# Two transformer blocks in one kernel: 64-column matmuls inside the 256-column projections, fillers among first tiles, and the second sparse selection spread over the first block's attention pieces

## What is computed

```python
def dsa_mixer(h, w_in, w_out, ...):
    q, k, v, qi, ki, wi = jnp.split(h @ w_in, cuts, axis=-1)
    ...
    logits = jnp.einsum('bthd,bsd->bths', qib, ki)
    score = jnp.einsum('bths,bth->bts', jax.nn.relu(logits), wib)
    _, sel = lax.top_k(jnp.where(visible, score, -jnp.inf), top_k)   # top_k = 64
    s = jnp.einsum('btgrd,btkgd->btgrk', qg, kg) * scale
    p = jax.nn.softmax(jnp.where(sel_ok, s, -jnp.inf), axis=-1)
    return jnp.einsum('btgrk,btkgd->btgrd', p, vg) @ w_out

def squared_relu_mlp(h, w_up, w_down):
    a = jax.nn.relu(h @ w_up)
    return (a * a) @ w_down

def swiglu(h, w1, w3, w2):
    return (jax.nn.silu(h @ w1) * (h @ w3)) @ w2
```

## Time and profile before

| | us |
|---|---|
| median of 3 runs | 1652.6 |
| the three runs | 1651.94, 1652.6, 1661.68 |
| the profiled execution, its own time | 1659.97 |
| its span | 1658.2 |
| PE busy in it (matmul) | 1611.2 |

### The profile page before, as it was taken

The page is one execution under the profiler, slowest core; times in us unless marked ns, Lnnn a source line. Parts: engine busy times, 40 slices in busy tenths (PEclk is TensorE's granted clock), DMA queues, the critical chain, the costliest instruction groups (busy, mean ns, idle before and its releaser), DMA issues.

```text
span 1658.2 us, 30920 instructions
## 1 busy us (share of the span) xinstructions
PE 1611.2 (97%) x12608; PEld 1535.0 (93%) x12608; DVE 1015.6 (61%) x1247; ACT 764.7 (46%) x1004; POOL 22.9 (1%) x39
## 2 busy tenths in 40 slices
PE   7989999999999999999999999999999999999999
PEld 5868999998999998999977999989999897889998
DVE  7786665568666546556467665466664657576653
ACT  4335554347655444444345444454443435554443
POOL 0000000004000000000000000000000000000000
PEclk9999999999999999999999999999999999899999
DMA  6701566644256665556623557635566351246573
GB/s 166 179 26 50 179 185 192 182 139 138 77 177 186 195 188 163 177 173 185 180 71 102 177 177 197 172 113 177 177 191 170 116 180 56 77 135 192 179 210 95
DMA packets 347106, 252.95 MB, mean 153 GB/s; under 512 B 32622, under 2 KB 345868, under 8 KB 347036
## 3 DMA queue, kind: packets, MB, share of 16 engines
q1 hardware_dynamic: 345424, 250.00, 51.2%
q10 hardware_dynamic: 1612, 1.97, 0.4%
HBM read 250.90 MB, written 1.05 MB: 152 GB/s over the span
## 4 chain that ended last, share of the span: by engine, by line
PE 86%; DVE 8%; ACT 2%; DMA 2%; issue 1%; ACTq 0%; SPq 0%; DVEq 0%
PE acc L531 26%; PE acc L533 25%; PE acc L532 25%; DVE w_low L1634 1%; ACT w_high L1147 1%; PE spare L714 1%; PE acc L556 1%; PE acc L736 1%; PE spare L556 1%; PE acc L722 1%; DVE xg_low L1678 1%; PE acc L1047 1%; DVE x_state L1841 1%; PE spare L588 1%; DVE evac_a L1839 1%
## 5 line engine op out<-in xcount | busy, mean ns | idle before, releaser
L1634 DVE TENSOR_TENSOR w_low<-w_raw,w_high 128x2048 fp32r<-128x2048 f32 (+2 forms) x222 | 528.6, 2381 | 381.9 <-ACT w_high L1147 381.9
L1147 ACT ACTIVATE w_high<-w_raw 128x2048 fp32r<-128x2048 f32 (+2 forms) x222 | 441.2, 1987 | 617.5 <-PE acc L533 598.6
L531 PE MATMUL acc<-xg_high,w_high 128*128 128x272 f32 (+2 forms) x2320 | 665.8, 287 | 13.3 <-DVE xg_low L1678 10.6
L533 PE MATMUL acc<-xg_high,w_low 128*128 128x272 f32 (+2 forms) x2320 | 657.4, 283 | 0.0
L532 PE MATMUL acc<-xg_low,w_high 128*128 128x272 f32 (+2 forms) x2320 | 657.4, 283 | 0.0
L531 PEld LDWEIGHTS acc<-xg_high,w_high 128*128 128x128 f32 (+1 forms) x2320 | 437.8, 189 | 23.6 <-issue 10.9
L532 PEld LDWEIGHTS acc<-xg_low,w_high 128*128 128x128 f32 (+1 forms) x2320 | 436.4, 188 | 2.5 <-issue 1.7
L533 PEld LDWEIGHTS acc<-xg_high,w_low 128*128 128x128 f32 (+1 forms) x2320 | 436.3, 188 | 0.2
L531 PE MATMUL acc<-hidden_high,w_high 128*128 128x256 f32 (+1 forms) x1216 | 343.7, 283 | 1.9 <-DVE w_low L1634 1.9
L533 PE MATMUL acc<-hidden_high,w_low 128*128 128x256 f32 (+1 forms) x1216 | 343.2, 282 | 0.0
L532 PE MATMUL acc<-hidden_low,w_high 128*128 128x256 f32 (+1 forms) x1216 | 343.1, 282 | 0.0
(11 more groups left out here) (284 smaller groups left out, 1455.1 us busy)
## 6 DMA issues: line engine op xcount, KB each, us to landing
w_raw<-in_ffn_w_dram SPq DMA_DIRECT2D x88, 1024.0 KB, 5.3
w_raw<-in_ffn_w_dram SPq DMA_DIRECT2D x32, 1408.0 KB, 6.9
w_raw<-in_mlp_w_up_dram SPq DMA_DIRECT2D x32, 1024.0 KB, 5.5
w_raw<-in_mlp_w_down_dram SPq DMA_DIRECT2D x32, 1024.0 KB, 5.5
w_raw<-in_attn_w_qkv_dram SPq DMA_DIRECT2D x12, 1024.0 KB, 5.1
w_raw<-in_a_w_in_dram SPq DMA_DIRECT2D x18, 256.0 KB, 4.4
w_raw<-in_a_w_in_dram SPq DMA_DIRECT2D x4, 1024.0 KB, 7.8
w_raw<-in_a_w_out_dram SPq DMA_DIRECT2D x4, 1024.0 KB, 5.0
```

Of the source, the lines that this page charges most:

```text
L531: pe.matmul(dst, high_w, high, start=first, stop=False)
L533: return pe.matmul(dst, low_w, high, start=False, stop=last)
L1147: act.activation(whi[slot(c)][:, 0:SIZES[c]], raw[c % 2][:, 0:SIZES[c]], ACT.Copy).then_inc(S["w_high"], 1)
L1634: dve.tensor_tensor(wlo[slot(c)][:, s], raw[c % 2][:, s], whi[slot(c)][:, s].bitcast(F32), ALU.subtract)\
```

## The change

- `short(tiles)`: one float32r matmul of 64 columns, stationary and moving operand from the tensor at hand, result unread. It stands after unit 0 in `a_out`, `b_out` and `w_o`, after unit 2 in `up` and after unit 1 in `down`, the last two only where the unit has 256 columns (MLP 0, MLP 1, FFN 3). So there are nine of them. `up` peels off units 2 and 3 for it.
- Fillers: in `sum_tiles` one `keep_busy` matmul of 256 columns after the first k-tile and two after the second (FFN 0 to 3 and `qkv`), one after each of the first three parts of the pooling projection, and two ahead of each of the last two transposes of the differential attention.
- Sparse attention: pieces go block 0 first, then block 1. Before them stands only block 0's selection; block 1's eight rounds stand among the first six pieces (2, 2, 1, 1, 1, 1). For block 0 the mask is added by PE (an identity matmul on `hide`), VectorE reads the maximum and ScalarE the exponential straight from `spare`, which is free again only at `exp_done`. The factor `A_SCALE` goes into the evacuation of q. The 30 early fillers become 16, and those beside the turns become 4, 4 and six times 1 of 128 columns. GpSimd copies the identity once at the start.

```diff
+            def short(tiles):
+                pe.matmul(sp[0][:, 1, 0:SHORT], tiles[:, 0:P], tiles[:, 0:SHORT], start=True, stop=True)
...
                 def beside(k):
+                    if k < 2:
+                        keep_busy(sp[0][:, 0], 1 + k, 256)
...
                 unit(1)
+                if T == SEQ:
+                    short(HH)
...
-                with pe.Fori(0, g.units // 2 - 1) as i:
-                    for j in range(2, 4):
+                for j in range(2, 4):
+                    wide(g, j, T0, T)
+                    if j == 2 and T == SEQ:
+                        short(XH[:, 0])
+                with pe.Fori(0, g.units // 2 - 2) as i:
+                    for j in range(4, 6):
...
                 def make_scores(p):
                     if p >= 2:
-                        pe.wait_ge(S["s_read"], s0 + p - 1)
+                        pe.wait_ge(*((S["exp_done"], e0 + p - 1) if masked(p - 2) else (S["s_read"], s0 + p - 1)))
...
+                def add_mask(p):
+                    ready, one, table, a, b = mask
+                    pe.wait_ge(*ready)
+                    for c in range(2):
+                        ins = pe.matmul(sp[p % 2][:, c, a:b], one, table, start=False, stop=True)
...
                         if p <= len(idle):
-                            keep_busy(acc[0][:, (p - 1) % 2], idle[p - 1], 256)
+                            keep_busy(acc[0][:, (p - 1) % 2], idle[p - 1], P)
...
-            attention([(i, m) for m in range(8) for i in range(2)],
+            attention([(i, m) for i in range(2) for m in range(8)],
...
-                      "exp_done", [2, 2, 1, 1], 2 * 15)
+                      "exp_done", [4, 4] + [1] * 6, 16,
+                      mask=((S["hide_ready"], 1), identA[:], hide[:, 0, 0:P], 0, P))
...
                 wide(g, j, META, SEQ, oT_waits() if j == 0 else None, high=OH, low=OL)
+                if j == 0:
+                    short(OH[:, 0])
...
+                if q < 3:
+                    keep_busy(normps, 1, 256)
...
                     make_scores(p + 2)
+                else:
+                    pe.wait_ge(S["c_probs"], p - 1)
+                    keep_busy(acc[0][:, p % 2], 2, 256)
...
+            def second_block(p):
+                if p < 6:
+                    take_eight(1, 2 if p < 2 else 1)
+                if p == 5:
+                    hide_rest(1)
+                if p == 7:
+                    dve.wait_ge(S["hide_ready"], 2)
+            take_eight(0, TOPK // 8)
+            hide_rest(0)
```

More of the change, by code:

```diff
@@ L47 @@
 DIFF_SCALE = HD ** -0.5
+SHORT = 64
 LAMBDA_INIT = 0.8 - 0.6 * math.exp(-0.3 * 1)
@@ L702, in turn_values, with attention, masked @@
                     ins.then_inc(S["v_turned"], 1)
-            def attention(pieces, scores, prob_tiles, values, probs_by, idle=(), early=0, values_in=0):
-                s0, t0, o0 = n.get("s_read"), n.get("pt_ready"), n.get("o_read")
+            def attention(pieces, scores, prob_tiles, values, probs_by, idle=(), early=0, values_in=0, mask=None):
+                s0, t0, o0, e0 = n.get("s_read"), n.get("pt_ready"), n.get("o_read"), n.get("exp_done")
+                def masked(p):
+                    return mask is not None and pieces[p][0] == 0
                 def make_scores(p):
                     if p >= 2:
-                        pe.wait_ge(S["s_read"], s0 + p - 1)
+                        pe.wait_ge(*((S["exp_done"], e0 + p - 1) if masked(p - 2) else (S["s_read"], s0 + p - 1)))
                     for c, (q, k) in enumerate(scores(*pieces[p])):
-                        ins = pe.matmul(sp[p % 2][:, c, 0:k.shape[1]], q, k, start=True, stop=True)
+                        ins = pe.matmul(sp[p % 2][:, c, 0:k.shape[1]], q, k, start=True, stop=not masked(p))
+                    if not masked(p):
+                        ins.then_inc(S["s_full"], 1)
+                    elif p >= 2:
+                        add_mask(p)
+                def add_mask(p):
[3 more added lines that the diff above has]
+                        ins = pe.matmul(sp[p % 2][:, c, a:b], one, table, start=False, stop=True)
                     ins.then_inc(S["s_full"], 1)
@@ L1320, in copy_v, with attention @@
                     act.activation(d, pieces, ACT.Copy).then_inc(S["v_ready"], 1)
-            def attention(pieces, keys, slots, outs):
+            def attention(pieces, keys, slots, outs, first=None):
                 s0, t0, o0 = n.get("s_read"), n.get("pt_full"), n.get("o_full")
@@ L1331, in exps @@
                     for c in range(2):
-                        ins = act.activation(Pr[p % 2][:, c, 0:nk], Sm[p % 2][:, c, 0:nk], ACT.Exp,
+                        ins = act.activation(Pr[p % 2][:, c, 0:nk], (first if first and pieces[p][0] == 0 else Sm)[p % 2][:, c, 0:nk], ACT.Exp,
                                              bias=rowneg[:, p % 4, c:c + 1], accum_out=rowsum[:, p % 4, c:c + 1])
@@ L1413, in _ @@
                 act.activation(Sm[q % 2][:, :, 0:nk], sp[q % 2][:, :, 0:nk], ACT.Relu).then_inc(S["idx_relu"], 1)
-            pieces = [(i, m) for m in range(8) for i in range(2)]
-            attention(pieces, lambda i: (i + 1) * P, lambda i: [(0, 2 * (i + 1), P)], None)
+            attention([(i, m) for i in range(2) for m in range(8)], lambda i: (i + 1) * P,
+                      lambda i: [(0, 2 * (i + 1), P)], None, sp)
             out_high(OH)
@@ L1478, in _ @@
             copy_v([(acc[(g.u0 + 2) % 2][:, i, :], vB[:, i, 512:D]) for i in range(2)])
-            attention(pieces, lambda i: (i + 1) * P, lambda i: [(0, 2 * (i + 1), P)], None)
+            attention([(i, m) for m in range(8) for i in range(2)], lambda i: (i + 1) * P,
+                      lambda i: [(0, 2 * (i + 1), P)], None)
             out_high(OH)
@@ L1735, in rope, with rope_unit @@
                     link(ins)
-            def rope_unit(g, j, rows_, tiles, r):
-                scaled(g, j, ta[(g.u0 + j) % 2][0:rows_, 0:tiles, 0:SEQ], rows_, tiles, r, SEQ)\
+            def rope_unit(g, j, rows_, tiles, r, scale=1.0):
+                unit_wait(g, j)
+                dve.scalar_tensor_tensor(ta[(g.u0 + j) % 2][0:rows_, 0:tiles, 0:SEQ],
+                                         acc[(g.u0 + j) % 2][0:rows_, 0:tiles, 0:SEQ], scale,
+                                         across(r[0:rows_, 0:SEQ], tiles), ALU.mult, ALU.mult)\
                     .then_inc(S["dve_evac"], 1)
@@ L1913, in ffn, with attention @@
                     post_norm(T0, T, gcol=gcol)
-            def attention(pieces, scale, keys, mask, outs, combine=None):
+            def attention(pieces, scale, keys, mask, outs, combine=None, beside_scores=None):
                 s0, e0, o0 = n.get("s_full"), n.get("exp_done"), n.get("o_full")
@@ L2071, in four_apart @@
                 return eight[:, :, m % 4]
-            attention(pieces, lambda i: A_SCALE, lambda i: (i + 1) * P, lambda i: hide[:, i, 0:(i + 1) * P], outs_of(four_apart))
+            attention([(i, m) for i in range(2) for m in range(8)], lambda i: 1.0, lambda i: (i + 1) * P,
+                      lambda i: hide[:, i, 0:(i + 1) * P].bitcast(F32) if i else None, outs_of(four_apart),
+                      beside_scores=second_block)
             out_low(OH, OL)
```

38 lines of the change are left out of this document (27 added, 11 removed).

## The result

The changed kernel takes 1641.16 us, median of four runs (1639.58 to 1641.76). The kernel before, beside it and with a fourth run, 1657.14 us (1651.94 to 1662.24). The ratio is 0.988, 95% interval 0.9841 to 0.9919. I forecast 1638.0 with a range of 1628 to 1649, and gave most of the chance to "within 1%", next to "faster by over 1%": the ratio lies just beyond that edge, on the faster side, but its interval covers the edge, the plain quotient of the two medians is 0.990, and 1641.16 is above the 1636.1 from which I had counted "faster". The same kernel in a later set of runs took 1647.57 us (ratio 0.9932, interval 0.9907 to 0.9957). So its gain is about 1%, and which side of the edge it falls on is not decided.

The account below looks back on a forecast made before the run. PE, at 97% share, was taken as the bound. Terms -10.0 + 0.5 - 4.8 - 6.0 + 1.8 + 0.9 = -17.6 us from the profiled 1659.97 gave 1642.4; less 4.4, 1638.0 us, range 1628 to 1649.

Parts of the forecast that it names:

- Two paces, one removed by the short matmul: 256-column streams: a 64-column matmul turns the slow pace, 117.6 ns, into the fast, 113.3 ns; -10.0 us.
- 3 units x 48 in each of `a_out` and `b_out`: Slow matmuls behind the short one in these output projections, counted as gaining 4.3 ns each, part of the 10.0 us.
- the price of the short matmul itself: Nine added matmuls on PE: 0.06 us each, between 0.03 and 0.12; +0.5 us in all.
- The first rival: 256-column streams: the short matmul does not move the pace, the 10.0 us are not won; 1648 us, chance 0.19.
- The third rival: `mlp_up0`, `mlp_up1`, `mlp_down1`: odd matmul throws fast streams slow, +7.8 us, and 10.0 not won; 1655.8 us, chance 0.05.
- Attention, -4.8: Sparse attention: block 0 first, starting earlier; piece 15's scores end near 129.9 instead of 134.66; -4.8 us.
- The clock, -6.0: Fillers avert half-clock stretches at 1096, 1304 and 1413 (`ffn_up2`, `qkv`, differential attention); -6.0 us, bounds 0 and 8.4.
- +0.9 for block 0: Sparse attention: PE idles a fifth of block 0's time, which may bring a half-clock stretch; +0.9 us (0 to 1.7).
- The fillers' price, +1.8: Fillers' own cost on PE: pooling projection +1.3, FFN 0 +0.4, differential attention 0.1; +1.8 us.
- The step to the median, -4.4: Whole kernel: the profiled execution lay 7.4 us above the median of 1652.6; 4.4 us of that taken off.
- All cured: Rival: every named half-clock stretch goes, no new one comes, full 7.4 us median offset stands; 1631.7 us, chance 0.32.

Follow-up runs that it names:

- before, again: The kernel before, unchanged, run again for a second trace: 1662.19 us, ratio 1.001.
- the two joined versions: Changed kernel plus short matmuls in 272-column parts, out_high moved 128 bytes, down's short matmul after unit 0: 1637.68 us; the same without pool fillers: 1637.56 us.
- set 1: Follow-up runs of short matmuls, new attention order and fillers, each alone, beside the kernel before, whose median there is 1661.4 us (31 runs).
- the first set: The original measurement, ahead of the follow-up sets: changed kernel 1641.16 us, kernel before 1657.14 us.
- set 3: Follow-up runs with the changed kernel again, 1647.57 us, beside the kernel before, 1661.3 us (15 runs).

## Why the prediction came out right, point by point

**Two paces, one removed by the short matmul: right in kind, 10.0 us was too much.** Summed by stage the trace shows 6.9 (3.0 - 0.7 + 0.1 + 3.1 + 1.4), and 3.0 of that is `mlp_down0`, which was fast already ahead of its short matmul: a lucky draw. The 0.7 lost in `mlp_down1` is an unlucky one, slow up to its short matmul where the kernel before was fast. The step that failed is "3 units x 48 in each of `a_out` and `b_out`": nothing there, 1.2 us, because of where out_high lies. The second is that faster PE work uncovers the weights. PE at the start of `ffn_down3`, changed kernel:

```profile
1568.41 0.28 PE L539 MATMUL acc<-xg_high,w_low 128*128 128x256 f32 x1
1569.83 0.36 PE L537 MATMUL acc<-hidden_high,w_high 128*128 128x256 f32 x1 [1.14 <-DVE w_low L1682]
```

Before, the second row's matmul began 0.56 us after the first's (1587.39 - 1586.83); now it is 1.42 (1569.83 - 1568.41), 1.14 of it idle, put down to w_low. The weights come from a transfer that lands at 1563.97, then ScalarE and VectorE split them; PE, through `ffn_up3` 3.9 us sooner, now gets there first. So `ffn_up3` gained 3.9 at its own pace and handed on 3.1. The third is the price of the short matmul itself. PE around the one in `mlp_down0`, changed kernel:

```profile
275.86 0.19 PE L566 MATMUL spare<-hidden_high 128*128 128x64 f32 x1
275.89 0.37 PE L537 MATMUL acc<-hidden_high,w_high 128*128 128x256 f32 x1
276.10 0.28 PE L538 MATMUL acc<-hidden_low,w_high 128*128 128x256 f32 x1
```

The next two matmuls begin 0.03 and 0.24 us after it, where without it they would begin 0 and 0.11 after that moment: 0.13 us. Summed in the same way over the eight starts around each of the nine it is 0.11 to 0.14 us each and 1.2 us in all, not 0.5. That is a little over the 0.12 that I had as its upper bound. Two executions of `mlp_down0`, fast throughout, say the same: 88.16 us with one (changed kernel) and 88.03 without (before, again).

**The first rival, a pace that isn't moved: refuted.** The same position in `mlp_down1` is slow ahead of the short matmul and fast behind it, FFN 3 went with the short matmul in every trace, and its width decides the way it goes. A neighbour of another width does leave a trace, for 100 us. The Trainium skill's "TensorE: Matmul & The Clock Gate", section "Back-to-back issue gap", beside which I had put this rival, gives one isolated gap per column count; in these streams there are two spacings, 113.3 and 117.6 ns.

**The third rival, slower: its mechanism is real, at another width.** At 64 columns no fast stream was thrown; at 128 and 256 they were, and the kernel with 256 was 7.5 us slower than the one with none, where this rival had +7.8 for the fast streams thrown. I had argued against it that fast stretches came through small waits unharmed. That was no argument: a wait is not an odd matmul. The 64 was the part of the edit that mattered, and nothing in the trace of before could tell it from 128.

**Attention, -4.8: right.** Up to `a_out` it measured 5.1. VectorE's first maximum, and PE's last scores and the transposes that follow the last division, changed kernel:

```profile
104.11 0.42 DVE L1981 TENSOR_REDUCE row_neg_max<-spare 128x2 f32<-128x256 f32 x1 [2.18 <-PE spare L745]
```

```profile
129.94 0.70 PE L735 MATMUL spare<-a_k,a_q 64*128 64x256 f32 x4
...
136.22 1.96 PE L799 MATMUL spare<-constants,attn_out 128*128 128x128 f32 x16 [0.46 <-DVE attn_out L2004]
```

The first maximum was to come at 102.8 and came at 104.11: PE ran the early fillers at half clock (below), which made them 1.6 us longer. Block 0 then took 13.4 us where I had worked out 14.3, and the scores of piece 15 end at 130.6 (129.94 + 0.70) against my 129.9 and the 134.66 of before. In the kernel with short matmuls in the 272-column parts too, whose early fillers ran at full clock, the first maximum is at 102.52 and `a_out` at 138.59; the 1.6 us between this and 140.17 is the stretch, and the ten traces with the new order fall into these two groups by it, five and five. The kernel before had a half-clock stretch too, in its transposes at 140. What that one is worth, the kernel with the fillers alone tells: it has the old order, and no stretch there. (It has one on the early fillers, at 94.4, which in the old order moved nothing: the transposes begin at 140.34 against 140.27.) PE, last transposes and first matmul of `a_out`, before and with the fillers alone:

```profile
140.27 3.54 PE L765 MATMUL spare<-constants,attn_out 128*128 128x128 f32 x16 [0.45 <-DVE attn_out L1950]
...
145.31 0.35 PE L531 MATMUL acc<-out_high,w_high 128*128 128x256 f32 x1
```

```profile
140.34 1.97 PE L767 MATMUL spare<-constants,attn_out 128*128 128x128 f32 x16 [0.45 <-DVE attn_out L1957]
...
144.30 0.35 PE L531 MATMUL acc<-out_high,w_high 128*128 128x256 f32 x1 [0.27 <-DVE out_low L1968]
```

The transposes are 1.6 us shorter, but `a_out` begins only 1.1 us sooner behind them (3.96 against 5.04), because PE then waits for VectorE's `out_low`. So of the 5.1 the order gave 4.05 (140.27 - 136.22, the starts of the transposes) and the absent stretch at 140 gave 1.1. Without the stretch on the early fillers the order gives 5.6 (the transposes begin at 134.63 in the kernel with 272-column short matmuls). My terms were off in two places that cancel: the order is worth 5.6 where I had 4.8, and its new stretch cost 1.6 where I had 0.9. The 1.1 from the stretch at 140 I had not counted at all.

**The clock, -6.0: right by the rows, with luck at the end of the differential attention.** Busy time by stretch, changed kernel, PE: early fillers of the sparse attention, the start of the second mixer's attention, `qkv`'s first units, the end of the differential attention:

```profile
94.40:97.60 3.20, 3.01 (x12) 0.50 0.00 0
391.40:394.60 3.20, 2.86 (x13) 0.50 0.45 157
1303.90:1307.40 3.50, 3.50 (x30) 1.00 0.02 5
1396.00:1413.00 17.00, 15.19 (x92) 1.00 0.01 1
```

The stretches of the earlier trace rows at 1096, 1304 and 1413 are gone. From the transposes of piece 13 to `w_o` the way was 15.51 us (1428.02 - 1412.51) and is 11.55 (1413.64 - 1402.09): 4.0 where I had 5.0. `ffn_up2` gained 2.0. With the 1.5 that the stretch at 1304 gave back, that is 7.5 us in this pair of traces, where I had 6.0. But it is a good draw: from the start of `qkv` to `w_o` six traces with these fillers take 122.6 us as here, three take 127.3 and one 129.8, for a stretch of 10 or 17 us at the end; the four without them take 125.5 to 128.1. The stretch of 1.7 us that I had put down at +0.9 for block 0 did come, in the fillers ahead of it rather than in its pauses, and in five of the ten traces with the new order. The fillers in the differential attention are misplaced. The wait of the earlier trace rows that was to be filled, changed kernel, PE:

```profile
1402.09 0.55 PE L1078 MATMUL acc<-constants,probs 128*128 128x128 f32 x3 [1.30 <-DVE probs L2305]
...
1403.42 1.13 PE L562 MATMUL acc<-constants,ones 128*128 128x256 f32 x4
```

The wait ahead of the transposes is still 1.30 us, since the fillers stand behind them. That the stretch went away here all the same is what was measured; which of the waits brings it on was not tried.

**The fillers' price, +1.8: right.** The pool's cost 1.4 us (105.84 - 104.41, the two joined versions), where 1.3 was worked out. Those in FFN 0 cost nothing visible (`ffn_up0` begins 137.29 us ahead of `ffn_down0` before and 137.31 now), where I had 0.4.

**The step to the median, -4.4: too large a word for three runs.** The kernel before varies by 17 us between executions of one set, so the 7.4 us between the profile and the median of three runs was a draw. Its median over 31 runs of set 1 is 1661.4, over the profiled 1659.97. Without that step the sum was 1642.4; the first set measured 1641.2, set 3 1647.6, and the step is smaller than what lies between these two. The forecast's 3 us to the first set are no proof of its terms, then. The stage table bears on them, and there the sum is 18.9 us from one profiled execution to the other against 17.6 forecast, with errors of 1 to 3 us in the terms that cancel: that the total came so near is in part luck.

**All cured: no.** `a_out` and `b_out` kept the slow pace, the stretch at 430 gave way to one at 391, and the one at the early fillers is new in this trace (the kernel with the fillers alone, in the old order, has one there too, at 94.4).

## What to carry to other kernels

Count the records of a steady stretch before trusting a mean duration: a stream of weight load and 256-column matmul that issues one per 117.6 ns instead of 113.3 is in a slow pace that held for whole projections here, and one 64-column matmul at its start made it fast for 0.13 us. The width matters: 256 columns made this kernel 7.5 us slower than no odd matmul, and 128 gained nothing (ratio 0.9957, against 0.9923 with none). Where it does nothing, try another place for the moving operand. Put fillers where PE waits for first tiles: there they cost nothing and no half-clock stretch came in ten of ten traces, while three in a stream without waits cost 1.4 us and averted nothing visible. Where pace and clock are drawn anew in each execution, three runs don't give a median to 1%: make ten or more of both kernels side by side, and read what differs between two traces of the same program before crediting an edit.

## What the runs showed of the hardware that had not been expected

- One and the same weight load and matmul have two lasting paces at granted clock 1.00: 113.3 and 117.6 ns for 256 columns, 123.3 and 126.7 for 272. Of the streams without an odd matmul some are drawn anew in each execution (`mlp_up0`, `mlp_down0`, `mlp_up1`, `mlp_down1`, `w_o`, `ffn_up1`), others came out the same in all traces (`ffn_up0` and FFN 3 slow).
- An odd matmul's width sets the pace of what follows: 64 columns fast (113.3 ns), 128 columns the other one, 256 columns slow (117.8 ns), outside `a_out` and `b_out`.
- In `a_out` and `b_out` the 64-column matmul did nothing until out_high, the moving operand, lay 128 bytes further on (117.6 to 112.9 ns). Why the place matters stays open.
- The granted clock falls to 0.50 for 3.4 us, at times for 7 to 17, at places that differ between executions of the same program. Such a stretch came on fillers too: in the changed kernel it began at 94.3 in the first trace, at the end of an idle of 1.38 us, and at 95.7 in the second, 0.5 us into the fillers behind that same idle. So fillers behind a wait don't exclude it.
